# A two-layer diffusion trunk on one core: layer 0's gate is computed apart from its shift and scale

## What is computed

```python
silu_c = jax.nn.silu(c)
silu_cc = jax.nn.silu(c_ctx)
for l in range(DEPTH):
    mod_x = (silu_c @ w_ada[l] + b_ada[l])[:, None, :]
    mod_c = (silu_cc @ w_ada[l] + b_ada[l])[None, None, :]
...
    shift_x, scale_x, gate_x = jnp.split(mod_x, 3, axis=-1)
    hx = _rmsnorm(x, g_pre) * (1.0 + scale_x) + shift_x
...
    x_new = x + gate_x * _rmsnorm(y, g_post)
```

## Time and profile before

| what | us |
|---|---|
| median of 3 runs (2592.25 to 2603.63) | 2599.12 |
| the profiled execution: its own time | 2598.11 |
| its span, first to last instruction | 2596.1 |
| PE busy / share of the span | 2490.1 / 96% |
| PE weight loads busy | 2086.3 / 80% |
| DVE busy | 1141.2 / 44% |
| ACT busy | 1114.5 / 43% |
| POOL busy | 1221.2 / 47% |

### The profile page before, as it was taken

One profiled execution on the slowest core, in us unless ns is written; L12 is line 12 of the kernel. 1 busy time (PEld: TensorE's weight loads), 2 busy tenths in 40 slices (PEclk: granted clock), 3 DMA queues, 4 the chain that ended last, 5 costly groups with the idle time before them and its releaser, 6 DMA issues.

```text
span 2596.1 us, 38839 instructions
## 1 busy us (share of the span) xinstructions
PE 2490.1 (96%) x12993; PEld 2086.3 (80%) x12993; DVE 1141.2 (44%) x1698; ACT 1114.5 (43%) x2329; POOL 1221.2 (47%) x996
## 2 busy tenths in 40 slices
PE   7888999999999999999999989999999999999998
PEld 1887987898888777787888778898888788888887
DVE  2453657394345432333343456691535423333322
ACT  2646564496212454434433443793214333343333
POOL 1567983122222378855555442122213455555554
PEclk9899999999999999999999999999999999999999
DMA  6346761100120255544433431001211333344333
GB/s 251 90 137 179 215 196 61 33 1 22 51 63 27 61 159 158 161 118 148 131 107 106 162 102 49 9 1 42 65 37 33 104 109 109 113 136 145 109 109 133
DMA packets 393274, 262.38 MB, mean 101 GB/s; under 512 B 16935, under 2 KB 365751, under 8 KB 391611
## 3 DMA queue, kind: packets, MB, share of 16 engines
q1 hardware_dynamic: 378944, 227.07, 29.8%
q10 hardware_dynamic: 14204, 33.67, 3.7%
HBM read 251.23 MB, written 9.45 MB: 100 GB/s over the span
## 4 chain that ended last, share of the span: by engine, by line
PE 82%; POOL 6%; issue 4%; DVE 4%; ACT 2%; DMA 1%; DVEq 0%; ACTq 0%; POOLq 0%; SPq 0%
PE ps L744 78%; POOL w_lo L640 4%; PE ps L936 2%; POOL w_lo L633 2%; DMA w_raw<-in_w_in 1%; DVE r_prev L2156 1%; DVE softmax_stats L2049 1%; PE ps L776 0%; DVE a_probT_lo L1792 0%; DMA w_ada<-in_w_ada 0%; DVE a_out_sum L1792 0%; PE ps L876 0%; ACT w_hi L1279 0%; PE ps L922 0%; ACT a_prob L1450 0%
## 5 line engine op out<-in xcount | busy, mean ns | idle before, releaser
L633 POOL TENSOR_TENSOR w_lo<-w_raw,w_hi 128x512 fp32r<-128x512 f32 x644 | 877.1, 1370 | 976.6 <-ACT w_hi L1279 970.7
L744 PE MATMUL ps<-hT_hi,w_hi 128*128 128x512 f32 (+1 forms) x2528 | 944.1, 373 | 42.1 <-POOL w_lo L640 17.0
L744 PE MATMUL ps<-hT_lo,w_hi 128*128 128x512 f32 (+1 forms) x2528 | 930.9, 368 | 0.0
L744 PE MATMUL ps<-hT_hi,w_lo 128*128 128x512 f32 (+1 forms) x2528 | 930.7, 368 | 0.0
L1279 ACT ACTIVATE w_hi<-w_raw 128x512 fp32r<-128x512 f32 x760 | 472.0, 629 | 927.0 <-PE ps L744 839.9
L744 PEld LDWEIGHTS ps<-hT_hi,w_hi 128*128 128x128 f32 x2528 | 480.2, 190 | 136.6 <-issue 14.2
L744 PEld LDWEIGHTS ps<-hT_hi,w_lo 128*128 128x128 f32 x2528 | 480.5, 190 | 78.8
L744 PEld LDWEIGHTS ps<-hT_lo,w_hi 128*128 128x128 f32 x2528 | 480.9, 190 | 75.1
L1792 DVE TENSOR_TENSOR merge_tmp<-merge_tmp,ps 128x512 f32<-128x512 f32 (+1 forms) x160 | 101.5, 634 | 660.0 <-PE ps L744 409.1
L640 POOL TENSOR_TENSOR w_lo<-w_raw,w_hi 128x512 fp32r<-128x512 f32 x116 | 155.5, 1365 | 42.3 <-ACT w_hi L1279 42.0
L1792 DVE TENSOR_TENSOR merge_tmp<-merge_tmp 128x512 f32<-128x512 f32 (+1 forms) x120 | 165.9, 1382 | 4.1
(11 more groups left out here) (272 smaller groups left out, 3001.0 us busy)
## 6 DMA issues: line engine op xcount, KB each, us to landing
w_raw<-in_w_in SPq DMA_DIRECT2D x476, 256.0 KB, 2.9
w_raw<-in_w_o_rest SPq DMA_DIRECT2D x112, 256.0 KB, 2.8
w_raw<-in_w_out SPq DMA_DIRECT2D x74, 256.0 KB, 2.6
w_ada<-in_w_ada SPq DMA_DIRECT2D x8, 1536.0 KB, 9.6
w_raw<-in_w_ada SPq DMA_DIRECT2D x48, 256.0 KB, 2.7
w_raw_more<-in_w_in SPq DMA_DIRECT2D x72, 128.0 KB, 2.5
w_raw<-in_w_o_attn SPq DMA_DIRECT2D x32, 256.0 KB, 2.8
w_raw<-in_dft_x SPq DMA_DIRECT2D x16, 256.0 KB, 2.7
```

Of the source, the lines that this page charges most:

```text
L633: eng.tensor_tensor(w_lo[:, r, :], raw[:, r, :], w_hi[:, r, :].bitcast(F32), ALU.subtract).then_inc(sem["w_split"], tally.up("w_split"))
L744: return eng.matmul(dst, lhsT, rhs, start=start, stop=stop)
```

## The change

Layer 0's shift and scale columns (the first 2048 of 3072) are loaded first, in 16 DMAs of 512 KB, two for each block of 128 rows, and multiplied by PE with 4 matmuls per block. Four further DMAs of 1 MB bring the gate's third to the columns 0 to 511 of the `hT` blocks, which are free until the latents. Later, between the context's attention and its convolution, DVE multiplies the gate's third with the conditioning numbers (a per-partition scalar) and adds over the 8 row blocks: for each of the 2 streams one `tensor_scalar` and seven `scalar_tensor_tensor` of 128 x 1024. PE sums over the partitions with 16 matmuls against a column of ones (`gate_columns`, after the last R tile), DVE adds the bias and multiplies by `norm_post`, PE turns the columns to a row (`turn_gate`), and ACT copies it out and sends it to HBM (`save_gate`). PE waits for that copy before the stage ends.

```diff
+        w_ada_head = at("w_ada_head", [P, 2, KT, SEQ], 0)
+        w_ada_tail = at("w_ada_tail", [P, KT // 2, 2 * D], Z)
...
+        def ada_part(k, half):
+            if k < KT // 2:
+                return w_ada_head[:, half, 2 * k:2 * k + 2, 512:1024]
+            return w_ada_tail[:, k - KT // 2, half * D:(half + 1) * D].rearrange("p (a n) -> p a n", a=2)
+        def gate_part(k):
+            return w_ada_head[:, :, k, 0:512].rearrange("p a (c n) -> p a c n", n=256)
+        def gate_acc(s):
+            return w_ada_head[:, 0, 4 * s:4 * s + 4, 512:768].rearrange("p (a c) n -> p a c n", a=2)
...
@@ SP @@
             def modulation(p):
+                w = a["w_ada"][p.layer]
                 for k in range(KT):
-                    ada(p.layer, k)
+                    if k > 1:
+                        eng.wait_ge(ada_in[k - 2], 32)
+                    for half in range(2):
+                        eng.dma_start(ada_part(k, half), w[k * P:(k + 1) * P, half * D:(half + 1) * D]...)
+                for k in range(0, KT, 4):
+                    eng.wait_ge(ada_in[KT - 2 + k // 4], 32)
+                    for half in range(2):
+                        eng.dma_start(w_ada_head[:, half, k:k + 4, 0:512], ...).then_inc(sem["gate_w_in"], 16)
...
@@ PE @@
-                    for n in range(6):
+                    for n in range(4):
...
+            def gate_columns():
+                eng.wait_ge(sem["gate_sum"], tally.take("gate_sum", 2))
+                for s in range(2):
+                    for c in range(KT):
+                        last = mm(ps[:, 1, 256 + s * KT + c:257 + s * KT + c], gate_acc(s)[...], small[:, 0:1], True, True)
+                last.then_inc(sem["gate_added"], tally.up("gate_added"))
...
                 project(p, 6)
+                if p.opens:
+                    gate_columns()
...
                 turn_values(p, R_V + 1, R_V)
+                if p.opens:
+                    turn_gate(1)
+                    eng.wait_ge(sem["gate_saved"], tally.take("gate_saved"))
                 stage_end(eng, tally, "pe")
...
@@ ACT @@
-                eng.dma_start(m_gpost[0:2, :], ...)
...
-                eng.wait_ge(sem["gate_made"], tally.take("gate_made"))
-                eng.dma_start(gate_rows[l], m_gate[0:2, :]).then_inc(sem["gate_out"], tally.up("gate_out", 16))
-                eng.wait_ge(sem["gate_out"], tally.now("gate_out"))
...
+                if p.opens:
+                    gate_tables(p.layer)
                 tile_range(p, A_Q, A_K)
...
                 tile_range(p, R_Q, R_Z)
+                if p.opens:
+                    save_gate(p.layer, 1)
                 stage_end(eng, tally, "act")
...
@@ DVE @@
-                for n in range(6):
+                for n in range(4):
...
-                tt(m_gate[0:2, :], m_rows[0:2, 2 * D:3 * D], m_gpost[0:2, :])...
...
+            def gate_sums():
+                eng.wait_ge(sem["gate_w_in"], tally.take("gate_w_in", 64))
+                for k in range(KT):
+                    for s in range(2):
+                        if k == 0:
+                            ins = eng.tensor_scalar(gate_acc(s), gate_part(0), sT[:, s, 0:1], None, ALU.mult)
+                        else:
+                            eng.wait_ge(sem["dve_own"], tally.now("dve_own", s - 1 if k == KT - 1 else -1))
+                            ins = eng.scalar_tensor_tensor(gate_acc(s), gate_part(k), sT[:, s, k:k + 1], gate_acc(s), ALU.mult, ALU.add)
...
                 attention(p)
                 stage_end(eng, tally, "dve")
+                if p.opens:
+                    gate_sums()
                 convolution(p)
...
                 r_keys(p)
+                if p.opens:
+                    gate_from_columns()
                 stage_end(eng, tally, "dve")
```

More of the change, by code:

```diff
@@ L974, in attention, with turn_gate @@
                         turn(g - 1, 1)
+            def gate_columns():
+                eng.wait_ge(sem["gate_sum"], tally.take("gate_sum", 2))
+                for s in range(2):
+                    for c in range(KT):
+                        last = mm(ps[:, 1, 256 + s * KT + c:257 + s * KT + c], gate_acc(s)[:, c // 4, c // 2 % 2, c % 2 * P:(c % 2 + 1) * P],
+                                  small[:, 0:1], True, True)
+                last.then_inc(sem["gate_added"], tally.up("gate_added"))
+            def turn_gate(bank):
+                eng.wait_ge(sem["gate_cols"], tally.take("gate_cols"))
+                eng.transpose(ps[0:2 * KT, bank, 0:P], n_gate[:, :, :], ident[:, :]).then_inc(
+                    sem["gate_turned"], tally.up("gate_turned"))
             def late_keys(after, p):
@@ L1879, in modulation, with gate_from_columns, gate_products @@
                 eng.wait_ge(sem["dve_own"], tally.now("dve_own"))
+            def gate_sums():
[7 more added lines that the diff above has]
+                            ins = eng.scalar_tensor_tensor(gate_acc(s), gate_part(k), sT[:, s, k:k + 1], gate_acc(s), ALU.mult, ALU.add)
+                        name = "gate_sum" if k == KT - 1 else "dve_own"
+                        ins.then_inc(sem[name], tally.up(name))
+            def gate_from_columns():
+                eng.wait_ge(sem["small_in"], tally.take("small_in", 32))
+                eng.wait_ge(sem["gate_added"], tally.take("gate_added"))
+                for s in range(2):
+                    tt(n_sum[:, s, 2 * KT:3 * KT], ps[:, 1, 256 + s * KT:256 + (s + 1) * KT], n_bias[:, 2 * KT:3 * KT], ALU.add).then_inc(
+                        sem["dve_own"], tally.up("dve_own"))
+                eng.wait_ge(sem["dve_own"], tally.now("dve_own"))
+                gate_products()
+            def gate_products():
+                for s in range(2):
+                    ins = tt(n_gate[:, s, :], n_sum[:, s, 2 * KT:3 * KT], n_post[:, :])
+                    ins.then_inc(sem["gate_cols"], tally.up("gate_cols")) if s else ins.then_inc(sem["dve_own"], tally.up("dve_own"))
             def mean(p, b):
```

55 lines of the change are left out of this document (23 added, 32 removed).

## The result

The changed kernel takes 2605.32 us (median of 16 runs, 2600.67 to 2612.91), the kernel before, run beside it, 2598.39 (16 runs, 2591.25 to 2606.70). The ratio is 1.003, with a 95% interval of 1.0018 to 1.0042: 5 to 11 us slower (6.9 by the medians), so within 0.5% of the kernel before, and a real loss. The profiled execution took 2600.89 us with a span of 2598.9 (before: 2598.11 and 2596.1).

The account below looks back on a forecast made before the run. PE, with 82% of the chain, was taken as the main bound. Opening -13.2, B tiles +13.1, columns +3.2 and turn +2.0 give +5.1 us on 2598.11, plus 1.0 for the median: 2604 us, 8-in-10 range 2590 to 2613.

Parts of the forecast that it names:

- The opening: Start of the kernel up to the tokens' projection: fewer matmuls and a smaller first block give 13.2 us, between 11.7 and 15.5.
- tokens 1.5 us sooner, 2.2 us lost: Opening: the context's tokens come 1.5 us sooner, yet their late scaling delays DVE's bias sums, losing 2.2 us.
- The opening is bound by the 48 matmuls: Opening of the kernel before: PE always has data, a block loading in 3.7 us while PE needs 5.2 us.
- The B tiles: Context's B tiles: 16 DVE instructions taking turns with POOL last 32.7 us and delay the next stage by 13.1 us.
- upper bound of 16 us: B tiles: largest cost, with all 16 instructions at 2.31 us and nothing given back in the tables.
- The columns: R tiles: PE's 16 one-column matmuls at 0.20 us each cost 3.2 us, between 1.6 and 6.4.
- The turn at the stage's end: End of the R tiles: DVE's four small instructions, PE's transpose, ACT's copy and DMA start cost 2.0 us, between 1.2 and 2.8.
- The sum: Whole kernel: -13.2 + 13.1 + 3.2 + 2.0 = +5.1 us, with bounds of -8.0 and +13.5.
- No turns: B tiles: DVE does not alternate with POOL, ends at 145.3, stage costs 4.7; sum -3.3, 2596 us; chance 15%.
- All hidden: B tiles: all new DVE work fits the 16.25 us idle, at 0.9 us an instruction; sum -8, 2591 us; chance 7%.
- The clock falling through the B tiles: TensorE drops to 1.2 GHz for the B units, perhaps on through R-tile units: +17, 2616 us; chance 12%.
- Slow loads: Opening: 512 KB loads in 2 KB runs move only 267 GB/s, PE ends 3 us later; sum +8, 2607 us; chance 5%.

Follow-up runs that it names:

- e4: Kernel before, with each opening load of 12 KB rows cut into six loads of 2 KB rows; 2604.84 us in one run.
- e3: Kernel before, loads unchanged, but 4 instead of 6 matmuls a block and the gate's matmuls and bias sums dropped; 2590.31 us in one run.
- e1: Changed kernel with only 2 of the gate's 16 VectorE instructions in the B tiles; median 2593.64 us, ratio to the kernel before 0.997.
- e2: Changed kernel with the gate's running sums in PSUM instead of SBUF, only the last pair writing SBUF; median 2590.89 us, ratio 0.9967.
- e8: Changed kernel with running sums in PSUM and the 16 column matmuls moved ahead of the R tiles; median 2586.25 us, ratio 0.9942.
- e9: Changed kernel with four matmuls of 512 columns in place of the 16 of one column; median 2606.39 us, ratio 1.0024.

## Why the prediction was right

2604.0 us were forecast, 2605.3 came, and the mechanism is the one forecast: the opening's gain is spent in the B tiles, and the columns and the turn make the loss. The sizes of the terms are another matter. Step by step:

- **The opening**, -13.2: measured -14.9, close to the upper bound of 15.5. The matmuls gave 13.8 as forecast (PE's block took 30.04 instead of 43.81 us), the smaller first block 0.7 instead of 1.2. The step that failed is "tokens 1.5 us sooner, 2.2 us lost": the scaling ran at 31.47, and VectorE then stood idle 5.8 us until PE's first bank at 38.65, so nothing was lost. The bias sums followed PE's banks 0.86 us apart (38.65, 39.51), which I had named as a sign that I am wrong. I carried the tokens' 15 us over from a trace whose other queue had rows of 12 KB; e4 shows that these loads' form made it. The rule that I weighed there, turns by packets (the Trainium skill, DMA: Bandwidth & Descriptors, "Queues, rings and completion order"), gave the right outcome. What I took for its refutation fits it, if the queue with packets of 11 KB had the longer turns; that reading is argued from the packets' sizes, and no run shows the turns themselves.
- **"The opening is bound by the 48 matmuls"** held for the kernel before. e3 shows how near the second bound was.
- **The B tiles**, +13.1: measured +12.9, and the terms hold too: 32.5 us for the sixteen instructions (110.47 to 142.95), where 32.7 were forecast, 2.23 us from sum to sum, and 9.43 us from the convolution's start to `r_decay`'s end (142.95 to 152.38), where 9.5 were forecast. e1 and e2 confirm it from both sides: take 14 sums away, or their second SBUF input, and it is gone. My upper bound of 16 us does not follow from its own words: sixteen at 2.31 end at 162.3, and with the 9.5 us behind them that is 17.4 us late. Nothing that was measured came near it.
- **The columns**, +3.2 with a bound of 6.4 "if the clock is at half": measured +4.9, of which 3.5 their own time and 1.4 the clock behind them. Their own time was about right; what the sum left out is the clock, which I had put into the bound only, and only for the columns themselves. It fell at their end and cost time in the unit behind.
- **The turn at the stage's end**, +2.0: measured +1.5 (2.11 us from the last values to the states, instead of 0.62).
- **Not in the sum**: the last 0.85 of the 7.2 us in the R tiles are neither columns nor turn. At the stage's start TensorE's clock was low for longer than in the kernel before (granted 0.57 and 0.58 from 152 to 160 us, against 0.59 from 156 to 160). e4, with the kernel before's code, was 1.1 us longer in this stretch, so these 0.85 us are not shown to be a cost of the change.
- **The sum**, +5.1: measured +5.2 at the states, where all four terms are in. That it is so near is partly luck: the opening gave 1.7 us more than forecast and the turn cost 0.5 less, while the columns with the clock behind them took 1.7 more and the rest of the R tiles 0.85. By the medians the loss is 6.9 us, with 5.1 forecast at the lower end of the interval.
- **The rivals.** No turns: 1.20 us a sum does occur, but only with one SBUF input (e2). All hidden: nearly so with the sums in PSUM (e2). The clock falling through the B tiles: it stayed at 1.00 until 152 us and was low in the R tiles after PE's pause, as it was before at 157 to 160. Slow loads: they moved 389 to 397 GB/s from 20 to 36 us. PE's block took 30.04 us where 32 matmuls of 0.86 us take 27.5, but the 2.5 us more stood in the kernel before as well (43.81 where 48 take 41.3), so the new form of the loads cost nothing there. The 341 GB/s that the Trainium skill gives for 1 MB (DMA: Bandwidth & Descriptors, "Bandwidth") was passed by loads of half that size, several of them in flight at once.

## What to carry to other kernels

An engine's idle time is worth what its neighbour leaves of it: 16.25 idle us of VectorE beside a busy GpSimd hold, by an estimate from these two prices, seven sums at 2.23 us with two SBUF inputs, and thirteen at 1.20 with one of them in PSUM. So look for free banks for the accumulator. Put small TensorE work where TensorE waits, not behind its last unit: the same 16 matmuls cost 4.9 us in one place, and in the other the R tiles' first `w_hi` came no later for them (140.38 without, 139.95 with). When matmuls go from a loop that loads as it computes, ask in the same step whether their bytes leave the critical loads as well: that was nearly half of the gain here.

## What I had not expected of the hardware

- TensorE's clock falls behind a run of one-column matmuls although the engine is counted busy throughout: 0.63 granted at 172 to 176 us in the changed kernel, 0.61 at 136 to 140 in e8, 1.00 behind four matmuls of 512 columns in the same place (e9), which took 3.03 us to the next start where the sixteen took 3.62. In e1 the sixteen took 4.22 us, and the granted clock was 0.92 from 156 to 160 us, with the columns from 156.51 on.
- The form of one queue's loads sets how long another queue's wait: two token tiles of 512 KB took 10.1 and 14.6 us beside rows of 12 KB, 6.2 and 7.8 beside the same bytes in rows of 2 KB and loads of 256 KB (e4).
- A two-input VectorE instruction of 128x1024 costs 2.23 us beside GpSimd if both inputs lie in SBUF, 1.20 if one lies in PSUM, wherever the result goes, and GpSimd's unit 2.23 or 1.27.
